# Moving the heads of stages into the preceding stage, and a second bank for projected halves

## The reference

```python
h = rmsnorm(x, norm_w) @ w_in           # columns of all branches and of their gates
# A: differential attention, 4 heads, full causal, lam from four small vectors
a = softmax(q1 k1 + alibi) - lam * softmax(q2 k2 + alibi)
ya = rmsnorm(a @ v, subln_w) * (1 - lam_init) * silu(ga)
# B: sliding window of 128, 4 heads on 2 key groups, a learned sink per head
yb = softmax([q k + alibi, sink])[:, :-1] @ v * silu(gb)
# C: 8 heads on 2 key groups: compressed blocks, 8 chosen blocks of 64, window of 512
yc = (g0 * compressed + g1 * selected + g2 * window) * silu(gc)
out = rmsnorm(x + concat(ya, yb, yc) @ w_out, final_norm)
```

## Time and profile before

| | |
|---|---|
| median of 3 runs | 958.89 us (956.51 to 960.07) |
| profiled execution, its own time | 960.75 us |
| its span | 959.0 us |
| PE busy | 842.4 us (88%) |
| DVE busy | 599.7 us (63%) |
| ACT busy | 433.2 us (45%) |
| POOL busy | 147.4 us (15%) |

### The profile page before, as it was taken

The page is one execution under the profiler, slowest core; times in us unless marked ns, Lnnn a source line. Parts: engine busy times, 40 slices in busy tenths (PEclk is TensorE's granted clock), DMA queues, the critical chain, the costliest instruction groups (busy, mean ns, idle before and its releaser), DMA issues. The chain is left out here.

```text
span 959.0 us, 19211 instructions
## 1 busy us (share of the span) xinstructions
PE 842.4 (88%) x7748; PEld 710.8 (74%) x7748; DVE 599.7 (63%) x1352; ACT 433.2 (45%) x974; POOL 147.4 (15%) x115
## 2 busy tenths in 40 slices
PE   4999999968999897778889995999999999539997
PEld 3899886747777676556778874888888888528885
DVE  5931210337888888455639974788887888584552
ACT  5521111125565565345524214677777777621221
POOL 0232000020312120020035300010110101131220
PEclk9999999979899899689989996999999999859999
DMA  7220235151413211331154205000040000222441
GB/s 265 94 110 1 82 110 137 44 147 44 122 57 121 73 61 45 85 100 42 41 140 119 67 35 157 3 2 2 3 177 2 3 2 3 65 91 68 140 139 50
DMA packets 31943, 73.04 MB, mean 76 GB/s; under 512 B 5104, under 2 KB 13680, under 8 KB 30832
## 3 DMA queue, kind: packets, MB, share of 16 engines
q1 hardware_dynamic: 31856, 71.83, 23.7%
HBM read 55.57 MB, written 16.25 MB: 75 GB/s over the span
## 5 line engine op out<-in xcount | busy, mean ns | idle before, releaser
L1623 DVE SCALAR_TENSOR_TENSOR n_probsT_low<-n_turned,n_probsT_high 128x512 f16<-128x512 f32 (+3 forms) x192 | 94.5, 520 | 14.6 <-ACT n_probsT_high L1573 12.0
L1563 ACT ACTIVATE n_probs<-n_probs,n_negated_max 128x640 f32<-128x640 f32 (+7 forms) x128 | 94.1, 735 | 18.5 <-DVE n_negated_max L1614 17.4
L1573 ACT ACTIVATE n_probsT_high<-n_turned 128x512 f16<-128x512 f32 (+3 forms) x192 | 81.3, 458 | 45.3 <-PE n_turned L631 43.1
L1678 PE MATMUL n_scores<-n_keys_high,stacks 128*128 128x256 f32 (+2 forms) x192 | 78.5, 409 | 11.6 <-DVE n_keys_low L1600 8.4
L631 PE MATMUL n_turned<-identity,n_probs 128*128 128x128 f32 x528 | 81.4, 278 | 0.1
L631 PEld LDWEIGHTS n_turned<-identity,n_probs 128*128 128x128 f32 x528 | 60.9, 142 | 6.8 <-issue 3.2
L1614 DVE CUSTOM_DVE_ANT_0 n_probs<-n_scores,n_bias_full 128x1024 f32<-128x1024 f32 (+3 forms) x64 | 48.3, 755 | 24.4 <-PE n_scores L1682 24.3
L154 POOL TENSOR_TENSOR w_low<-w_raw,w_high 128x1024 fp32r<-128x1024 f32 x15 | 38.2, 2546 | 161.9 <-ACT w_high L147 161.6
L1679 PE MATMUL n_scores<-n_keys_low,stacks 128*128 128x256 f32 (+2 forms) x192 | 62.9, 334 | 0.0
L1659 POOL TENSOR_TENSOR branches_b_c<-branches_b_c,n_out 128x512 f32<-128x512 f32 x16 | 20.4, 1275 | 260.7 <-DVE n_out L1635 260.7
L554 PE MATMUL nat<-stacks,xT_high 128*128 128x256 f32 (+1 forms) x192 | 55.1, 287 | 3.0 <-DVE stacks L436 2.6
(11 more groups left out here) (259 smaller groups left out, 2566.3 us busy)
## 6 DMA issues: line engine op xcount, KB each, us to landing
w_raw<-in_w_feat SPq DMA_DIRECT2D x23, 512.0 KB, 3.6
features<-staged SPq DMA_DIRECT2D x30, 256.0 KB, 2.0
a_raw<-features SPq DMA_DIRECT2D x42, 128.0 KB, 2.7
branches_b_c<-in_x SPq DMA_DIRECT2D x8, 512.0 KB, 5.1
silu_gates<-staged SPq DMA_DIRECT2D x16, 256.0 KB, 2.0
s_raw<-features SPq DMA_DIRECT2D x16, 256.0 KB, 4.2
w_out_raw<-in_w_out SPq DMA_DIRECT2D x4, 1024.0 KB, 8.8
o_gatesT<-silu_gates SPq DMA_DIRECT2D x8, 512.0 KB, 4.8
```

The source lines that it names most:

```text
L1563: nc.scalar.activation(pr[:, n % PS, 0:w], pr[:, n % PS, 0:w], ACT.Exp, scale=-1.0, bias=nmax[:, hb % 4, qt:qt + 1], accum_out=sums[:, hb ...
L1573: nc.scalar.activation(pth[:, g % GS, 0:k, :], tp[g % TS][:, 0:k, :], ACT.Copy, scale=PSCALE).then_inc(t_high, 1)
L1623: nc.vector.scalar_tensor_tensor(out=ptl[:, g % GS, 0:k, :], in0=tp[g % TS][:, 0:k, :], scalar=PSCALE, in1=pth[:, g % GS, 0:k, :], op0=ALU ...
L1678: nc.tensor.matmul(out, q, kh[:, br, keys], start=True, stop=False)
```

## The change

**Start stage and A.** The twelve transfers of the first two heads' halves (`a_raw`), the four high parts and the low parts of `a_stack` are issued in the start stage: on SP behind the second hidden unit's signal, on ACT ahead of the last evacuation of a left half, on DVE (queries) ahead of the last evacuation, on POOL (keys) behind the value slabs. A begins with scores(0), and half 0 stands behind them.

The core of the diff:

```diff
+                if c == WITH_HIDDEN:
+                    sp.wait_ge(hidden, 2)
+                    for h in range(2):
+                        sp.wait_ge(f_out[h], 16 * WITH_HIDDEN)
+                    for j in range(4):
+                        src = feat_dram[(QA, KA)[j % 2][0], A_QK * (j // 2):A_QK * (j // 2 + 1), :]
+                        for band in range(3):
+                            sp.dma_start(a_raw[A_QK * band:A_QK * (band + 1), j, :], src).then_inc(a_raw_in, 16)
             for h in range(2):
...
+            def a_stack(j):
+                act.wait_ge(a_raw_in, 16 * 12)
+                nc.scalar.activation((qs, ks)[j % 2][:, j // 2, :], a_raw[:, j, :], ACT.Copy,
+                                     scale=A_QK ** -0.5 / slope4(0) if j % 2 == 0 else 1.0).then_inc(a_high, 1)
...
+                    for j in range(4):
+                        a_stack(j)
                 evacuate(c)
...
+                    for j in range(0, 4, 2):
+                        dve.wait_ge(a_high, j + 1)
+                        q_low = qs[A_QK:2 * A_QK, j // 2, :]
+                        nc.vector.scalar_tensor_tensor(out=q_low, in0=a_raw[A_QK:2 * A_QK, j, :],
+                                                       scalar=A_QK ** -0.5 / slope4(0), in1=q_low.bitcast(F32),
+                                                       op0=ALU.mult, op1=ALU.subtract)
                 evacuate(c)
...
+            pool.wait_ge(v_third, NV * NT)
+            for j in range(1, 4, 2):
+                pool.wait_ge(a_high, j + 1)
+                k_low = ks[2 * A_QK:K, j // 2, :]
+                nc.gpsimd.tensor_tensor(k_low, a_raw[2 * A_QK:K, j, :], k_low.bitcast(F32), ALU.subtract)
...
-                    sp.dma_start(raw_of(j)[A_QK * band:A_QK * (band + 1), :], src).then_inc(raw_in[2 if j in (2, 3) else j % 2], 16)
-
-            for j in range(LOADS):
-                load_raw(j)
...
             for m in range(2):
                 scores(0, m)
+            fill.project(pe, 0, range(KT))
             fill.project(pe, 1, range(KT))
             for m in range(2):
                 scores(1, m)
...
-    SS, TS, GS = 3, 2, 4
+    SS, TS, GS = 2, 2, 4
...
+        fb = [ctx.enter_context(nc.psum_tensor(f"b_projected{i}", [P, 512], F32)) for i in range(2)]
...
+            fill.gate_tanh(act, 1)
             exponentials(0)
-            exponentials(1)
-            fill.gate_tanh(act, 1)
             for n in range(UN):
-                if n + 2 < UN:
-                    exponentials(n + 2)
+                if n + 1 < UN:
+                    exponentials(n + 1)
                 high_part(n)
                 if stack_at(n):
...
+            fill.gate_out(dve, 1)
             dve.wait_ge(bias_in, 16)
             add_bias(0)
             add_bias(1)
-            fill.gate_out(dve, 1)
-            add_bias(2)
             for n in range(UN):
-                if n + 3 < UN:
-                    add_bias(n + 3)
+                if n + 2 < UN:
+                    add_bias(n + 2)
...
             scores(0)
             scores(1)
-            fill.project(pe, 1, range(KT))
-            scores(2)
             for n in range(UN):
-                if n + 3 < UN:
-                    scores(n + 3)
+                if n + 2 < UN:
+                    scores(n + 2)
                 fill.project(pe, *half_at(n))
                 turn(n)
...
+    CONSTS = 16 * 5
+    SPLIT_AT = (GU + 8, GU + 24, 6 * HU + 4)
+    ROOT_AT = 2 * NT
...
-            load_stack(0)
             sp.dma_start(bw[:, :], dist_win).then_inc(bw_in, 16)
             load_stack(1)
-            sp.dma_start(bf[:, :], dist_full).then_inc(bf_in, 16)
-            sp.dma_start(blk_in[:, :], blocks).then_inc(blk_loaded, 16)
+            sp.dma_start(bf[:, :], dist_full).then_inc(consts_in, 16)
+            sp.dma_start(blk_in[:, :], blocks).then_inc(consts_in, 16)
             load_stack(2)
             load_stack(3)
-            sp.wait_ge(scored, GU)
-            for s in range(SLABS):
-                sp.dma_start(w_out_raw[:, s, :], w_out[s]).then_inc(w_loaded, 16)
-            sp.wait_ge(w_loaded, 16 * SLABS)
+            sp.dma_start(sub[:, :], subln.partition_broadcast(P)).then_inc(consts_in, 16)
+            for i in range(2):
+                sp.dma_start(gates[:, i, :, :], gate_dram[:, :, i * P:(i + 1) * P].rearrange("k p n -> p k n")).then_inc(consts_in, 16)
+            sp.wait_ge(k_ready, 3)
+            for s in range(SLABS + 1):
+                if s >= 1:
+                    sp.wait_ge(w_low, s)
+                sp.dma_start(raw[:, :, :], w_out[s]).then_inc(w_loaded, 16)
+            sp.wait_ge(w_loaded, 16 * (SLABS + 1))
...
+            def split(s):
+                act.wait_ge(w_loaded, 16 * (s + 1))
+                act.wait_ge(scored, GU if s < 2 else 6 * HU)
+                nc.scalar.copy(stacks[:, 2 * s:2 * s + 2, :], raw[:, :, :]).then_inc(w_high, 1)
+
+            def a_roots():
+                act.wait_ge(a_vector, 3)
+                nc.scalar.activation(arms[:, :], arms[:, :], ACT.Sqrt, scale=small[:, 1:2], bias=small[:, 2:3]).then_inc(a_root, 1)
...
-            stack(0)
+            exponentials(0)
             stack(1)
-            exponentials(0)
-            act.wait_ge(blk_loaded, 16)
+            act.wait_ge(consts_in, CONSTS)
             nc.scalar.copy(blk[:, :], blk_in[:, :]).then_inc(mask_ready, 1)
             for n in range(UN):
...
+                if n == ROOT_AT:
+                    a_roots()
+                if n in SPLIT_AT:
+                    split(SPLIT_AT.index(n))
...
+            def a_sums(half):
+                dve.wait_ge(a_pool, half + 1)
+                cut = slice(NT // 2 * A_H * half, NT // 2 * A_H * (half + 1))
+                nc.vector.tensor_reduce(arms[:, cut], blk_in[:, :].rearrange("p (h d) -> p h d", d=HD), AX.X,
+                                        ALU.add).then_inc(a_vector, 1)
...
+            a_squares(0)
+            a_squares(1)
             for hb in range(UN // NT):
                 pool.wait_ge(headed, hb + 1)
                 if hb % 2 == 1:
                     pool.wait_ge(added, hb)
                 out = y_of(hb // 2)
                 nc.gpsimd.tensor_tensor(out, out, red[:, hb % 2, :, :], ALU.add).then_inc(added, 1)
+                if hb == 1:
+                    a_norm()
+                for s in range(SLABS):
+                    if SPLIT_AT[s] // NT == hb + 1:
+                        split(s)
...
-            sp.dma_start(sub[:, :], subln.partition_broadcast(P)).then_inc(rows_in, 16)
-            load_gates(0)
-            sp.dma_start(fn[:, :], final_row.partition_broadcast(P)).then_inc(rows_in, 16)
-            load_gates(1)
             load_x(0)
             load_x(1)
+            sp.dma_start(fn[:, :], final_row.partition_broadcast(P)).then_inc(rows_in, 16)
...
+            nc.scalar.copy(wh[:, KT - 2:KT, :], raw[:, :, :]).then_inc(w_high, 1)
+            high_part(0)
             for i in range(NT):
-                if i + 2 < NT:
-                    a_rstd(i + 2)
                 if i + 1 < NT:
                     high_part(i + 1)
...
-            for s in range(SLABS):
-                dve.wait_ge(w_high, s + 1)
-                cols = slice(s * W, (s + 1) * W)
-                nc.vector.scalar_tensor_tensor(out=wl[:, :, cols], in0=raw[s], scalar=0.5, in1=wh[:, :, cols].bitcast(F32),
-                                               op0=ALU.mult, op1=ALU.subtract).then_inc(w_low, 1)
-                if s == 0:
-                    a_norm(0)
-                    gate(0)
-            a_squares(1)
-            a_norm(1)
+            gate(0)
+            dve.wait_ge(w_high, 1)
+            nc.vector.tensor_tensor(wl[:, KT - 2:KT, :], raw[:, :, :], wh[:, KT - 2:KT, :].bitcast(F32),
+                                    ALU.subtract).then_inc(w_low, 1)
+            dve.wait_ge(rows_in, 16)
             for i in range(NT):
                 if i + 1 < NT:
                     gate(i + 1)
-                if i + 2 < NT:
-                    a_squares(i + 2)
-                    a_norm(i + 2)
...
-                for h in halves:
+            def project(i, ks):
+                for h in range(2):
                     n = 2 * i + h
-                    if n >= 4:
+                    if n >= 4 and ks[0] == 0:
                         pe.wait_ge(added, n - 3)
-                    if i == 0:
-                        pe.wait_ge(w_low, SLABS // 2 * (h + 1))
                     cols = slice(512 * h, 512 * h + 512)
-                    for k in range(KT):
+                    for k in ks:
...
-                    mm.then_inc(done, 1)
+                    if ks[-1] == KT - 1:
+                        mm.then_inc(done, 1)
             turn(0)
             turn(1)
-            project(0, (0, 1))
+            pe.wait_ge(low, 1)
+            project(0, range(0, 4))
+            pe.wait_ge(low, 2)
+            project(0, range(4, KT - 2))
+            pe.wait_ge(w_low, 1)
```

(4 more changed lines are left out.)

255 lines of the change are left out of this document (128 added, 127 removed).

## The result

The changed kernel took 932.33 us (median of 4 runs, 929.73 to 934.59), the kernel before 957.7 us in the same series. The ratio is 0.9734 with a 95% interval of 0.9707 to 0.9762, and the medians lie 25.4 us apart. The forecast was 932.6 us. The profiled execution had a span of 932.5 us and a mean granted clock of 0.946 (before: 0.935).

A forecast was written before the change was run, and what follows sets the result against it. TensorE bounds the kernel inside stages and idles at their heads (four waits, 50.7 us). Terms 21 + 12 + 3 - 4.7 - 5 = 26.3 us off the median of 958.89 give 932.6 us; range 922 to 943.

The forecast's parts named there:

- E, forecast 21: Last stage: first product starts at 836.8 (835.8 to 838.2) instead of 858.6, less 1 us; gain 21 us (19 to 23).
- The term for the low clock: Stage E: low clock after the first product, 2.1 us before, may last twice that with the earlier gap; 1 us more.
- B, forecast 12: Stage B: turn(0) 7.9 us earlier, 5.3 of waits between halves and 1.2 of low clock saved, 2.4 charged; gain 12 us.
- The charge of 2.4 us: Stage B: 1.5 us for shorter look-ahead in units 1 to 5 with stacks, 0.9 for possible low clock at the head.
- Start and A, forecast 3: Stacks moved ahead of A: A starts 4.2 us later, scores(1) follows after 15.8 us instead of 22.9; gain 3 us.
- Head of D, forecast -4.7: Stage D's head: ACT's block-mask cast waits for five loads, including gate tiles, so scores(5) comes later; loss 4.7 us (2.5 to 7).
- Rest of D, forecast -5: Inside D: root with table loads at unit 16, 2.4 us; three splits, 0.4, 0.4, 1.3; DVE 0.5; loss 5 us.
- the longer pause at the table loads: Rival, unit 16 of D: each table switch holds ACT another 1.28 us, costing TensorE 2.6 us; 935.2 us, chance 0.12.
- The look-ahead rival: Stage B: units with a stack, copy or write-out cost 0.7 us each, B keeps 4 us; 940.6 us, chance 0.13.
- the slower case: Stage B: every turn waits for its exponential with two score banks; at 1.0 us a unit 964 us, chance 0.03.
- The start-stage rival: Start stage: stacks cost more than they save, by DVE and POOL ordering and load collisions; A -4, 939.6 us, chance 0.07.
- Early loads: Rival, stage D: the five loads come early and insertions hide; head -3, inside D 0; 926 us, chance 0.14.

## Why the prediction was right

The mechanism named for each stage was the one that the rows show, and the time was right to 0.3 us. That close a hit is luck: four executions of the changed kernel spread over 4.9 us, a fourth run of the kernel before took its median from 958.89 to 957.7 us (so that the gain is 25.4 us where 26.3 was forecast), and errors cancelled. By the table, B and A gave 2.9 us more than forecast, E, C and the head of D 3.2 less.

- **E, forecast 21, measured 19.3.** The start of the first product was nearly right (4.9 us behind the stage's start forecast, 5.4 measured), but where it stood before was read from the chain as 858.6, and the timeline has 858.21: 20.9 us gained there, 21.8 forecast. The term for the low clock was too small: 1 us was charged on the assumption that the low stretch at most doubles from 2.1 us. It went from 2.6 to 6.0 us in this profile, 8 products more at 0.43 us in place of 0.23, which cost 1.6 us. The gap ahead of the first product had become shorter and the low stretch longer, so a shorter gap doesn't by itself mean an earlier high clock. Of the range's two ends, GpSimd first was seen as forecast (3.9 us); with VectorE first it was 5.4 to 5.9 us and not 6.3.
- **B, forecast 12, measured 14.3.** The head was right: `turn(0)` comes 8.0 us earlier (7.9 forecast), 17.7 us behind the start. The waits for the halves' bank with the low clock behind them gave 7.1 us (6.5). The charge of 2.4 us was mis-sized: the shorter look-ahead cost 0.9 us and not 1.5, and the 0.9 us for a low clock behind the gap at the head didn't come.
- **Start and A, forecast 3, measured 3.6 in this pair, some 2 over all profiles.** Counted from TensorE's last product, A begins 7.7 us later where 3.3 stood: 4.4 us, 4.2 forecast. The other 2.2 us of its later start lie in the first 100 us of this execution (the third weight chunk was issued at 102.29 and not at 100.02; it was at 100.18 in another kernel with the same start stage). scores(1) came 15.4 us behind A's start (15.8 forecast). The collision of VectorE and GpSimd was there, but one reading of it was wrong, see below.
- **Head of D, forecast -4.7, measured -5.4.** The named instruction, its releaser and its size were right, and the run with the mask's own semaphore turns the loss into a gain.
- **Rest of D, forecast -5, measured -4.5.** The root cost more (3.4 us over its units, 2.9 forecast with VectorE's part: 46.91 - 43.47), the splits less (the adds lose 1.0 us from unit 66 on, 2.1 forecast).
- **C, forecast 0, measured -0.8**, within what C varies by.

Of the rivals, the longer pause at the table loads falls: each switch took its 1.28 us and the next instruction followed within 0.02 us, TensorE lost 2.68 us and not 5. The Trainium skill, ScalarE: Activation LUTs, section What ACT_TABLE_LOAD costs, counts 1.38 us of drain for each switch besides; the rows at unit 16 show none. The look-ahead rival and the slower case, both of B, fall with the 1.52 us units of the changed kernel and the 0.9 us above. The start-stage rival, a loss of 4 us there, falls by the run with the stacks back in A. Early loads fall with the 10.79 us wait.

The rule that carried a term, the Trainium skill's in GPSIMD Engine Reference, section 1 Specifications (GpSimd shares its SBUF interfaces with VectorE, which then contends in a 2-port mode or with two SBUF inputs), agrees with the rows here: 2.61 us for 1.22, 3.59 for 0.18, and 0.18 again once GpSimd's product was moved. The rows also show that the later of the two waits for the earlier to end. That already stood in the trace before, where the prediction took 2.41 us against 2.20 for a slight stretch of an instruction that takes 2.20 by itself. Both were held until GpSimd's instructions ended at 212.83 and 215.29. First GpSimd beside the second of them, then the same VectorE instruction in the changed kernel, where GpSimd is idle:

```profile
212.91 2.38 POOL L154 TENSOR_TENSOR w_low<-w_raw,w_high 128x1024 fp32r<-128x1024 f32 x1
```

```profile
211.65 0.19 DVE L864 CUSTOM_DVE_ANT_0 a_lam_vectors<-a_lam_vectors 128x32 f32<-128x32 f32 x1 [8.23 <-DMA a_lam_vectors<-in_lams]
```

Its term came out right all the same, as it went by turns and not by a stretch.

Not settled: what decides the length of E's low stretch from run to run, and how the 2 to 5 us by which some medians go beyond their steps divide between the edits and the clock.
